# Query and key projections of the second attention: as 24 ordinary products of the front stage, or as side products inside the first attention

## What is computed

```python
def attn_mixers(h, positions, w_in, rel_bias, diff_lam, diff_norm_g, w_out, lambda_init):
    q_c, k_c, v_c, q_idx, k_idx, w_idx, q_d, k_d, v_d = split_cols_2(h @ w_in, CD_SIZES)
    # per block of 128 queries:
    rel = einsum('bqhd,bsd->bqhs', q_idx, k_idx)               # 8 index heads of 32
    score = einsum('bqhs,bqh->bqs', relu(rel), w_idx) * scale_idx
    sel = top_k(where(causal, score, -inf), 128)               # the keys that the first attention may see
    out_c = softmax(q_c k_c * scale_c + bias_c[bucket(dist)], over sel) v_c           # 8 heads of 64
    b_d = bias_d[bucket(dist)]
    attn = softmax(q1 k1 * scale_d + b_d) - lam * softmax(q2 k2 * scale_d + b_d)      # 4 heads, two maps each
    out_d = rmsnorm(attn v_d) * (1 - lambda_init)
    return concatenate([out_c, out_d]) @ w_out
```

## Time and profile before

| | us |
|---|---|
| median of three runs | 3900.58 |
| runs, lowest to highest | 3891.02 to 3908.12 |
| the profiled execution, own time | 3888.52 |
| its span | 3886.8 |
| busy in the span: PE, DVE, ACT, POOL | 3362.7, 1581.8, 701.0, 196.9 |
| mean granted TensorE clock | 0.929 of full |

### The profile page before, as it was taken

How to read it: one execution, slowest core, us unless ns; L and a number is a source line. 1 busy time by engine, 2 the same in 40 slices (tenths; PEclk the granted TensorE clock), 3 DMA queues, 4 the chain that set the end, 5 groups by cost and what they waited for, 6 DMA issues and landing times. The chain is left out here.

```text
span 3886.8 us, 42440 instructions
## 1 busy us (share of the span) xinstructions
PE 3362.7 (87%) x16176; PEld 1625.0 (42%) x16177; DVE 1581.8 (41%) x3043; ACT 701.0 (18%) x1412; POOL 196.9 (5%) x263
## 2 busy tenths in 40 slices
PE   8998998888899999988889788779599878688775
PEld 4454443774445443377334432223343344322222
DVE  3335556664324555666456400000258774100002
ACT  2132303100113321400011100000132353000001
POOL 0001010001000001000100000000100230000000
PEclk9999999989999999998899899999799999799998
DMA  2214462004211245200522499999333321999996
GB/s 95 83 38 171 152 214 63 13 2 149 85 55 49 65 143 159 55 2 2 197 87 83 203 428 428 428 428 357 124 106 120 99 66 53 387 427 421 429 428 275
DMA packets 208103, 696.55 MB, mean 179 GB/s; under 512 B 22248, under 2 KB 105704, under 8 KB 182736
## 3 DMA queue, kind: packets, MB, share of 16 engines
q1 hardware_dynamic: 178576, 589.42, 39.7%
q0 software_dynamic: 29376, 105.05, 7.5%
HBM read 636.14 MB, written 58.28 MB: 179 GB/s over the span
## 5 line engine op out<-in xcount | busy, mean ns | idle before, releaser
L347 PE MATMUL bank<-fm,w 128*128 128x512 f32 (+1 forms) x912 | 399.7, 599 | 14.7 <-DMA w<-in_ab_w_in 8.3
L2816 PE MATMUL bank<-experts_wu,experts_hs 128*64 128x512 f32 x1120 | 279.9, 658 | 71.0 <-DMA experts_wu<-in_moe_w_up 70.9
L2816 PE MATMUL bank<-experts_wg,experts_hs 128*64 128x512 f32 x1120 | 271.2, 640 | 61.6 <-DMA experts_wg<-in_moe_w_gate 47.9
L347 PE MATMUL bank<-w,fm 128*128 128x512 f32 (+2 forms) x768 | 316.6, 568 | 6.6 <-DMA w<-in_w_in 6.6
L2881 DVE TENSOR_TENSOR fm<-bank,fm 128x512 f32<-128x512 f32 x35 | 37.0, 1056 | 645.8 <-PE bank L2816 645.8
L2816 PE MATMUL bank<-experts_wd,fm 128*64 128x512 f32 x1120 | 257.6, 614 | 43.3 <-ACT fm L2865 23.1
L347 PEld LDWEIGHTS bank<-fm,w 128*128 128x128 f32 (+1 forms) x912 | 173.2, 191 | 238.7 <-issue 222.6
L728 PE MATMUL bank<-fm,side_w 128*128 128x512 f32 x512 | 250.3, 614 | 6.8 <-DMA side_w<-in_w_in 5.4
L347 PEld LDWEIGHTS bank<-w,fm 128*128 128x128 f32 x768 | 143.9, 198 | 178.8 <-issue 153.3
L2816 PEld LDWEIGHTS bank<-experts_wu,experts_hs 128*64 128x64 f32 x1120 | 86.5, 150 | 262.4 <-issue 170.0
L2816 PEld LDWEIGHTS bank<-experts_wg,experts_hs 128*64 128x64 f32 x1120 | 94.8, 147 | 234.0 <-issue 230.9
(11 more groups left out here) (487 smaller groups left out, 4579.9 us busy)
## 6 DMA issues: line engine op xcount, KB each, us to landing
experts_wg<-in_moe_w_gate SPq DMA_DIRECT2D x64, 2048.0 KB, 19.5
experts_wu<-in_moe_w_up SPq DMA_DIRECT2D x64, 2048.0 KB
experts_wd<-in_moe_w_down SPq DMA_DIRECT2D x64, 2048.0 KB
ada_w<-in_ada_w POOLq DMA_DIRECT2D x96, 512.0 KB, 4.8
w<-in_w_in SPq DMA_DIRECT2D x40, 512.0 KB, 3.9
expert_rows<-fm POOLq DMA_DIRECT2D x35, 512.0 KB, 10.3
fm<-expert_rows SPq DMA_DIRECT2D x33, 512.0 KB, 21.6
w<-in_w_in SPq DMA_DIRECT2D x16, 1024.0 KB, 7.2
```

The source lines that it names most:

```text
L347: ins = pe.matmul(bank, lhsT, rhs, start=(n == 0), stop=(n == len(todo) - 1))
L2816: ins = pe.matmul(bank[rows, :], lhs[:, k, rows], weights[:, s, k, cols], start=(k == 0), stop=(k == chunks - 1))
```

## The change

The eight heads jobs for q_d and k_d leave the front stage. In their place the first attention gets eight side products: each multiplies 128 columns of the weights (one head with its two maps) by all 512 tokens and gives the result feature-major, which is the shape that `turn_qk` made, so the second attention has `turned_in=True` and turns nothing. The scale of q is put on when ACT moves the side product (`side_scales`). The front's 64 bias jobs stand after 10 heads jobs in place of 16, seven each and one after the last. The turned blocks of the first attention use the second half of `y_fm` (`scratch_at`). The sigmoid that follows the side products in the first block is left out when there are side scales.

```diff
-    fills = 2 if packed else 4
+    fills = 0 if turned_in else 2 if packed else 4
...
         def turned(which, m, a):
 
+            if turned_in:
+                return (q, k)[which][:, m, :]
             return turned_sb[(m % 2) * n_turned + 2 * (0 if packed else a) + which]
+
+            def load_side(sp, n):
+                if n >= 2:
+
+                    sp.wait_ge(*side_summed.at(n - 1))
+                sp.dma_start(side_w[n % 2][:, :, :], side_jobs[n][0].rearrange("(k p) n -> p k n", p=P)
+                             ).then_inc(*side_loaded[n % 2].inc(16))
...
                             sp.dma_start(bias_sb[g % ring][rows, a, :, :], src[:, 2 * (g % 2):2 * (g % 2) + 2, :]
                                          ).then_inc(*loaded[g % ring][a].inc(16))
+                    if g < n_side:
+                        load_side(sp, g)
...
-                if i == 0:
+                if i == 0 and not turned_in:
...
-                    act.activation(side_jobs[n][1], SIDE[:, :], ACT.Copy).then_inc(*side_moved.inc())
+                    act.activation(side_jobs[n][1], SIDE[:, :], ACT.Copy, scale=side_scales[n] if side_scales else 1.0
+                                   ).then_inc(*side_moved.inc())
...
-        for names, dsts in ((("q_c", "k_c", "v_c"), topk), (("q_d", "k_d", "v_d"), diff)):
+        for names, dsts in ((("q_c", "k_c", "v_c"), topk), (("v_d",), (diff_v,))):
...
             if n < 6:
                 add_scores(4)
-            elif n < 22:
-                add_biases(4)
+            else:
+                add_biases(min(7, PAIRS - len(biased_at)))
...
-                          scale=HD ** -0.5, bias=bias_of, masks=masks)
+                          scale=HD ** -0.5, bias=bias_of, masks=masks,
+                          side=(fm, [(io["cd_w_in"][0][:, CD[name] + c * P:CD[name] + (c + 1) * P], dst[:, c, :])
+                                     for name, dst in (("q_d", diff_q), ("k_d", diff_k)) for c in range(DIFF_HEADS)]),
+                          scratch=y_fm, scratch_at=DIFF_HEADS * SEQ, side_scales=[HD ** -0.5] * DIFF_HEADS + [1.0] * DIFF_HEADS)
...
-            attention(chip, "diff_attention", q, k, lambda m, j: vd[:, j, m, :], HD, mixed, causal=False, scale=HD ** -0.5,
+            attention(chip, "diff_attention", diff_q, diff_k, lambda m, j: vd[:, j, m, :], HD, mixed, causal=False, turned_in=True,
```

More of the change, by code:

```diff
@@ L619, in attention @@
 def attention(chip, name, q, k, v, dk, out, gate=None, causal=True, scale=1.0, bias=None, masks=None, mix=None, decay=None,
-              side=None, cleared_rows=None, scratch=None, early=None):
+              side=None, side_scales=None, turned_in=False, cleared_rows=None, scratch=None, scratch_at=0, early=None):
     steps, pairs = HEADS * TILES, HEADS // 2
@@ L628, in attention @@
     packed = dk <= HD
-    fills = 2 if packed else 4
+    fills = 0 if turned_in else 2 if packed else 4
     with chip.stage(name) as st:
         n_turned = 2 * (1 if packed else 2)
-        if scratch is None:
+        if turned_in:
+            turned_sb = []
+        elif scratch is None:
             turned_sb = [st.sb(f"turned{i}", [P, SEQ]) for i in range(2 * n_turned)]
         else:
-            turned_sb = [part(scratch, i * SEQ, SEQ) for i in range(2 * n_turned)]
+            turned_sb = [part(scratch, scratch_at + i * SEQ, SEQ) for i in range(2 * n_turned)]
         prob = [st.sb(f"prob{i}", [P, SEQ]) for i in range(4)]
@@ L659, in turned, with _ @@
         def turned(which, m, a):
+            if turned_in:
+                return (q, k)[which][:, m, :]
             return turned_sb[(m % 2) * n_turned + 2 * (0 if packed else a) + which]
+        if side:
+            side_w = [st.sb(f"side_w{i}", [P, DC, P]) for i in range(2)]
+            side_loaded = [st.count(f"side_w{i}_loaded") for i in range(2)]
+            side_summed, side_moved = st.count("side_summed"), st.count("side_moved")
+            def load_side(sp, n):
[3 more added lines that the diff above has]
+                             ).then_inc(*side_loaded[n % 2].inc(16))
+            if bias is None:
+                @st.block.sync
+                def _(sp):
+                    for n in range(n_side):
+                        load_side(sp, n)
         if bias is not None:
@@ L697, in _ @@
                 pool.wait_ge(*wiped.at(wiped.total))
[L699 to L710, removed]
         if early is not None:
@@ L857, in _ @@
                 act.wait_ge(*side_moved.at(n_side))
-            for n in range(n_side):
+            for n in range(n_side if side_scales is None else 0):
                 act.activation(side_jobs[n][1], side_jobs[n][1], ACT.Sigmoid)
@@ L2231, in conv_mixers, with attn_front @@
         routed.programs()
-def attn_front(chip, io, fm, mod, scratch, topk, diff, causal, masks, ex, lambda_init):
+def attn_front(chip, io, fm, mod, scratch, topk, diff_v, causal, masks, ex, lambda_init):
     w_in = io["cd_w_in"][0]
@@ L2440, in attn_mixers @@
         with ExitStack() as diff_heads:
-            diff = [sb(f"diff_{n}", [P, TILES, 2 * DIFF_HEADS, HD], diff_heads, side="right") for n in "qkv"]
+            diff_q, diff_k = (sb(f"diff_{n}", [P, DIFF_HEADS, SEQ], diff_heads, side="right") for n in "qk")
+            diff_v = sb("diff_v", [P, TILES, 2 * DIFF_HEADS, HD], diff_heads, side="right")
             with ExitStack() as topk_heads:
                 topk = [sb(f"topk_{n}", [P, TILES, HEADS, HD], topk_heads, side="right") for n in "qkv"]
-                attn_front(chip, io, fm, mod, scratch, topk, diff, causal, masks, ex, lambda_init)
+                attn_front(chip, io, fm, mod, scratch, topk, diff_v, causal, masks, ex, lambda_init)
                 y_fm = sb("y", [P, DC, SEQ])
@@ L2447, in attn_mixers @@
                 attention(chip, "topk_attention", q, k, lambda h, j: v[:, j, h, :], HD, y_fm, causal=False,
-                          scale=HD ** -0.5, bias=bias_of, masks=masks)
+                          scale=HD ** -0.5, bias=bias_of, masks=masks,
+                          side=(fm, [(io["cd_w_in"][0][:, CD[name] + c * P:CD[name] + (c + 1) * P], dst[:, c, :])
+                                     for name, dst in (("q_d", diff_q), ("k_d", diff_k)) for c in range(DIFF_HEADS)]),
+                          scratch=y_fm, scratch_at=DIFF_HEADS * SEQ, side_scales=[HD ** -0.5] * DIFF_HEADS + [1.0] * DIFF_HEADS)
             mixed = sb("mixed", [P, DIFF_HEADS, SEQ])
-            q, k, v = diff
-            vd = v[:, :, :, :].rearrange("p t (h a) d -> p t h (a d)", a=2)
-            attention(chip, "diff_attention", q, k, lambda m, j: vd[:, j, m, :], HD, mixed, causal=False, scale=HD ** -0.5,
+            vd = diff_v[:, :, :, :].rearrange("p t (h a) d -> p t h (a d)", a=2)
+            attention(chip, "diff_attention", diff_q, diff_k, lambda m, j: vd[:, j, m, :], HD, mixed, causal=False, turned_in=True,
                       bias=lambda m: bias_of(HEADS + m), masks=causal, mix=ex[:, 2:3])
```

## The result

The change takes 3914.16 us, the median of 18 runs (3895.20 to 3929.86), beside 3895.37 for the kernel before in 18 runs on the same chip. The ratio is 1.0041, 95% interval 1.0028 to 1.0053: 16 us slower by the ratio (the two medians lie 18.8 apart), within 0.5% of no change. The forecast was +16.

A forecast was written before the change was run, and what follows sets the result against it. Front bound by PE with DVE 24.2 us behind, first attention by no engine alone, second by DVE. -19.0 + 37.5 - 2.5 = +16, read against the median of 3900.6: 3916 us, range 3900 to 3934.

The forecast's parts named there:

- The front, -19.0: Front stage: 21.6 us less with heads jobs removed, less a clock charge of 2.6; bounds -22 and -9.5.
- 24.2 us of waits: Front: DVE's waits for PE add up to 24.2 us; PE work taken out beyond that brings nothing.
- hitch of 0.8 us: Front, each cycle: DVE's step 10 held behind a heads job, at 2907.1 where free running gives 2906.3; cycle 17.0 us.
- clock charge of 2.6: Front: PE's clock falling in each cycle's thin part slows heads jobs; 2.6 us taken between bounds 0 and 12.
- The first attention, 119.8: First attention: PE becomes the bound, 52.4 us of its own plus 56.5 of projections plus ends; +37.5, bounds +28 and +42.
- 26.4 of slack: First attention: slack less its ends that the 56.5 us of moved work would go into.
- rival 4: Each engine's load evens out: front down 56.5 us, attention up 56.5 less PE's idle 29.9; -32, 3869 us; chance 0.03.
- The second attention, -2.5: Second attention: transposes and moves gone, three DVE copies worth 2.0 us and PE waits 0.5; between -4.5 and 0.
- The first is not on the path: Second attention: DVE's first copy saves nothing, since the first maximum waits 4.0 us for the mask in any case.
- 1, the clock swings in the front: Thin part of each front cycle: whole clock charge of 12 us paid, front -9.6, sum +25, 3926 us; chance 0.17.
- 2, a dearer first attention: First attention: late exponentials and three banks make DVE and PE take turns, 8 us more; +24, 3924 us; chance 0.12.
- 3, ends hidden better: Ends hidden better and the clock holds: front -21.6, attention +32, sum +8, 3908 us; chance 0.10.

The follow-up runs named there:

- half version: Against before: only q_d by four side products, k_d feature-major in the front, five bias jobs per projection; 3885.6 us, ratio 0.9958; timed again 3884.4, 0.9974.
- ring of four: Front's ring of steps four deep instead of three: on the change, front 150.6 us, 3909.4 in one execution; on the kernel before, front 180.1, ratio 1.0008.
- attempt to show it above: The change plus seven unread matmuls on PE after the second attention's first four scores; that stage 71.6 us, 3923.4 in one execution.
- thin version: The change with only the first of each side product's eight matmuls made in the first attention; that stage 85.9 us, 3886.3 in one execution.
- both mends: Half version plus ring of four and first side weights sent after half of the bias loads: 3873.9 us, ratio 0.9951; same two on the change: 3897.0, 1.0010.

## Why the prediction was right, and where it was not

**The front, -19.0; measured -15.6 and -17.3.** That DVE would be late next was right: the half version shows the same front for half the work moved. That the 24.2 us of waits were all that could be had was wrong: with a ring of four the front gave 28.5 to 29.6, since DVE was also done 9.4 us ahead of the stage's end. The sum itself did not use the 24.2 but followed the steps to the end, and that held: the stage ends 12.4 us after its last step begins (12.1 forecast). What was short is the hitch of 0.8 us in each cycle: it shows as waits of 1.07, and the undisturbed cycle is 17.2 us where 17.0 was said, 1.8 us over eight. The clock charge of 2.6 measured 4.0 in one execution (two low projections, 1.62 + 2.38) and 2.4 in the other (one). The ring of four takes nearly all of both away together, and with them the front is 14 us shorter. The signs named for the front, waits of about 8 us and 158 to 161 us, were both missed: 15.4 and 13.7, 164.5 and 162.9.

**The first attention, 119.8; measured 121.8 and 118.8.** Adding up PE's own work was the right method: a steady pass was 13.6 in the sum and took 13.4. The weights came 11.7 and 9.0 us after the stage's start for 9 in the sum; that is the whole difference between the two executions. More of the start ran low (0.50 in the first 10 us of the first), against which the rest ran a little quicker. (The sum's "26.4 of slack" and the 29.9 of rival 4 are one idle time, 82.3 - 52.4 = 29.9.) What failed is the other end of the subtraction: +37.5 took 82.3 for before from one execution. On the means of two executions after and of four with before's order it is 120.3 less 85.6, +35. Of the signs, 120 us and the one wait of 5 us came; the clock near 1.0 did not (0.94 and 0.95).

**The second attention, -2.5; measured 0.** This term was wrong. "The first is not on the path" held exactly: before, DVE waits 4.0 for the mask, 2.3 for a turn and copies 0.7; after, it waits for the mask alone (groups by line):

```profile
L895 DVE CUSTOM_DVE_ANT_0 bank<-bank,bias 128x512 f32<-128x512 f32 x32 | 22.1, 693 | 8.8 <-POOL bias L710 7.0 <-PE bank L764 1.8
L919 DVE SCALAR_TENSOR_TENSOR prob<-prob,sums 128x512 f32<-128x512 f32 x16 | 19.8, 1238 | 0.6
```

The other three copies, 2.0 us, were counted as gained, and "some PE waits go: 0.5" besides. Instead waits for scores grew: 1.8 us on the mean of the eleven executions without turns (0.7 to 3.2), 0.7 on the mean of the three with them. The operation that mixes two maps (L907, now L919) took 20.1 against 19.5 on these means, but it wanders from 18.1 to 21.5 without turns and from 19.2 to 20.1 with them, so its part is not shown. The two together are about the 2.0 us of the copies. With the turns PE had work at the start of the stage; now its second scores are

```profile
3189.95 2.74 PE L764 MATMUL bank<-attn_diff_k,attn_diff_q 64*128 64x512 f32 x4 [6.28 <-ACT prob L857]
```

and the clock is low until 3205, 24 us into the stage (before: 16; windows after):

```profile
3191.60:3197.60 6.00, 4.96 (x13) 2.04 (x11) 5.76 (x16) 3.10 (x8) 1.53 (x1) 0.50 0.26 87
3197.60:3205.60 8.00, 7.01 (x22) 4.24 (x22) 7.59 (x19) 4.49 (x12) 2.35 (x1) 0.55 0.22 67
```

That this is why the scores are late is argued, not shown; the attempt to show it above only moved the fall.

**The sum.** On these means, -16.5 + 35 + 0 = +18 against +16 forecast and +16 measured. The three errors of 2 to 3 us are +2.5, -2.5 and +2.5; two of them cancel, so the right total is partly luck.

**The rivals.** 1, the clock swings in the front: half true in kind, false in size. One or two of eight projections began low, in five executions with this front (164.5, 162.9, 164.5, 162.9, 164.4), where it took four to decide the sign. In one of the five a further fall touched the bias jobs alone and cost 0.7 us. The Trainium skill ("TensorE: Matmul & The Clock Gate", A second HAM failure mode) describes this swing. The trace agrees that it happens, at 1.6 to 2.4 us for each low projection, and not that it sets the time: most of the gaps passed without one. 2, a dearer first attention: it did not come, since a steady pass took 13.4 us without a gap on PE; the thin version adds that loads, moves and three banks cost nothing by themselves. 3, ends hidden better: they were not. 4, even loads: refuted, and the half version shows what is right in it. Where PE has slack, 28.2 us of work cost 9 to 10 (8 with both mends); beyond that slack, the next 28.2 cost 24 to 26.

## What to carry to other kernels

Taking work from the bounding engine pays only down to the next engine's slack, which is its waits and the stretch at the stage's end in which it is already done: read both first and move that much, not all. Where the slack is cashed, the next wait can be a buffer's depth, which here was worth nothing while DVE was ahead and 14 us once it was late. Where one engine works through a stage without a gap, what is left to win is how soon it can start. Before subtracting a stage's length, take a second execution.

## What the hardware did that was not expected

The same order of instructions doesn't get the same clock or time: the first attention without side products, PE busy for 76 to 77% of it, took 82.3, 85.7, 85.7 and 88.7 us at mean clocks of 0.88, 0.84, 0.84 and 0.85. The first and one of the two of 85.7 are the same kernel. The longest did not have the lowest clock, so the clock is not all of it, and the rest stays open. The full clock also didn't last: after 10 us at 1.00 with PE 99% busy, a stretch with 4.38 us of work in 6.2 had 0.75, and the next, 4.92 in 6, had 0.50.
